# The norms of a hybrid decoder trunk: mean squares spread by one matrix product with a tile of 1/1024

## The reference, cut to what matters

```python
def rmsnorm(x, g):
    xf = x.astype(jnp.float32)
    y = xf * lax.rsqrt(jnp.mean(xf * xf, axis=-1, keepdims=True) + EPS)   # EPS = 1e-6
    return (y * g.astype(jnp.float32)).astype(x.dtype)

for l in range(DEPTH):                                                    # DEPTH = 2
    h = h + 0.5 * swiglu(rmsnorm(h, ffn1_norm[l]), ffn1_w_in[l], ffn1_w_out[l])
    u = rmsnorm(h, mix_norm[l])
    q_a, c_kv, iq, ik, iw, z_pool, q_c, gate_pre = jnp.split(u @ w_in[l], split_pts, axis=-1)
    c_kv = rmsnorm(c_kv, kv_norm[l])                                      # 128 wide
    y_a = dsa_attention(...)      # an indexer scores the keys, top 128 are attended to
    y_b = pool_mixer(...)
    y_c = mem_attention(q_c, rmsnorm(mem, mem_norm[l]), w_mem_kv[l])      # 256 memory tokens
    h = h + (gated sum of the three branches) @ w_out[l]
    h = h + 0.5 * swiglu(rmsnorm(h, ffn2_norm[l]), ffn2_w_in[l], ffn2_w_out[l])
return rmsnorm(h, final_norm)
```

## Time and profile before

| | |
|---|---|
| median of three runs | 2257.93 us (2256.59 to 2258.37) |
| the profiled execution, its own time | 2256.72 us |
| its span in the trace | 2254.9 us |
| PE, matmul busy | 2209.5 us, 98% of the span, 10328 instructions |
| DVE busy | 963.2 us, 43% |
| ACT busy | 548.4 us, 24% |
| POOL busy | 1320.7 us, 59% |
| granted TensorE clock, mean | 0.996 |

### The profile page before, as it was taken

How to read it: one execution, slowest core, us unless ns; L and a number is a source line. 1 busy time by engine, 2 the same in 40 slices (tenths; PEclk the granted TensorE clock), 3 DMA queues, 4 the chain that set the end, 5 groups by cost and what they waited for, 6 DMA issues and landing times.

```text
span 2254.9 us, 31688 instructions
## 1 busy us (share of the span) xinstructions
PE 2209.5 (98%) x10328; PEld 1813.3 (80%) x10328; DVE 963.2 (43%) x1803; ACT 548.4 (24%) x1030; POOL 1320.7 (59%) x868
## 2 busy tenths in 40 slices
PE   7999999999999999999999999999999999999996
PEld 5888888778788888888788888888778888888885
DVE  4331345478754532023433222536877454321334
ACT  3110112443553211001121101215445432100111
POOL 5666667544436666666756666675444366666663
PEclk9999999999999999999999999999999999999998
DMA  6243323221213222322323332232121132323322
GB/s 173 101 131 105 100 77 120 89 71 62 67 56 99 94 93 88 101 100 85 108 98 120 105 110 94 78 121 82 61 71 64 50 112 94 99 83 107 101 78 72
DMA packets 67524, 209.81 MB, mean 93 GB/s; under 512 B 7368, under 2 KB 10600, under 8 KB 67176
## 3 DMA queue, kind: packets, MB, share of 16 engines
q1 hardware_dynamic: 63600, 202.84, 27.4%
q10 hardware_dynamic: 3832, 5.77, 1.1%
HBM read 204.91 MB, written 3.67 MB: 93 GB/s over the span
## 4 chain that ended last, share of the span: by engine, by line
PE 93%; DVE 4%; issue 1%; ACT 1%; DMA 0%; POOL 0%; DVEq 0%; ACTq 0%; POOLq 0%
PE bank L550 29%; PE bank L552 28%; PE bank L551 28%; PE obank L790 1%; PE sbank L735 1%; PE tbank L757 1%; DVE picks L1289 1%; DVE top L1287 1%; PE obank L568 0%; PE obank L562 0%; PE sbank L727 0%; PE sbank L710 0%; PE obank L774 0%; PE sbank L688 0%; PE sbank L741 0%
## 5 line engine op out<-in xcount | busy, mean ns | idle before, releaser
L504 POOL TENSOR_TENSOR wL<-raw,wH 128x1024 fp32r<-128x1024 f32 (+3 forms) x432 | 913.9, 2116 | 36.1
L501 POOL TENSOR_SCALAR wH<-raw 128x1024 fp32r<-128x1024 f32 (+3 forms) x432 | 406.9, 942 | 872.3 <-PE bank L552 858.5
L550 PE MATMUL bank<-u0H,wH 128*128 128x512 f32 x1408 | 551.4, 392 | 6.3 <-POOL wL L504 4.1
L552 PE MATMUL bank<-u0L,wH 128*128 128x512 f32 x1408 | 548.8, 390 | 0.0
L551 PE MATMUL bank<-u0H,wL 128*128 128x512 f32 x1408 | 548.8, 390 | 0.0
L550 PEld LDWEIGHTS bank<-u0H,wH 128*128 128x128 f32 x1408 | 265.0, 188 | 64.8 <-issue 8.7
L551 PEld LDWEIGHTS bank<-u0H,wL 128*128 128x128 f32 x1408 | 264.9, 188 | 55.5 <-issue 1.0
L552 PEld LDWEIGHTS bank<-u0L,wH 128*128 128x128 f32 x1408 | 264.9, 188 | 55.2
L550 PE MATMUL bank<-u1H,wH 128*128 128x512 f32 x704 | 293.3, 417 | 4.7 <-DVE u1L L1488 2.7
L552 PE MATMUL bank<-u1L,wH 128*128 128x512 f32 x704 | 275.2, 391 | 0.0
L551 PE MATMUL bank<-u1H,wL 128*128 128x512 f32 x704 | 274.9, 390 | 0.0
(11 more groups left out here) (174 smaller groups left out, 2140.1 us busy)
## 6 DMA issues: line engine op xcount, KB each, us to landing
raw<-in_wA SPq DMA_DIRECT2D x176, 512.0 KB, 3.2
raw<-in_wM SPq DMA_DIRECT2D x96, 512.0 KB, 3.3
raw<-in_wB SPq DMA_DIRECT2D x64, 384.0 KB, 3.0
raw<-in_wB SPq DMA_DIRECT2D x64, 320.0 KB, 2.9
raw<-in_wR SPq DMA_DIRECT2D x32, 256.0 KB, 2.6
h<-in_xT ACTq DMA_DIRECT2D x4, 512.0 KB, 7.3
mem<-in_memT SPq DMA_DIRECT2D x2, 1024.0 KB, 6.9
near_bias<-bias_rows ACTq DMA_DIRECT2D x2, 1024.0 KB, 7.0
```

The lines of the kernel that those rows point to most:

```text
L501: pool.tensor_scalar(wH[:, w, 0:cols], raw[:, slot, 0:cols], 1.0, 0.0, ALU.mult, ALU.add).then_inc(rounded, 1)
L504: pool.tensor_tensor(wL[:, w, 0:cols], raw[:, slot, 0:cols], wH[:, w, 0:cols].bitcast(F32), ALU.subtract).then_inc(split_done, 1)
L550: pe.matmul(dst, a, hi[:, k, :], start=first and i == 0, stop=False)
L552: mm = pe.matmul(dst, a, lo[:, k, :], start=False, stop=last and i == len(tiles) - 1)
```

## The change

One product takes the place of the two. A tile filled with 1/1024 (over_d; 1/128 for the latents, over_r) is the weights, and ssq itself, 128 x 512, the moving operand, so that obank holds the mean squares of all tokens on every partition. ACT takes the root of the whole 128 x 512 with EPS as a bias, straight into the destination; DVE takes the reciprocal in place and makes the correction with three scalar_tensor_tensor over 128 x 512. Row sums, diagonals and the copy go. Three memsets on DVE at the start fill the constant tiles, and PE and ACT wait for them, ACT before its first DMA of h. In norm 3 the product stands behind unit 1, no longer behind unit 0; in norm 4 it stays behind ("in", 2), but all of DVE's part moves to ("in", 3); in norm 2 all of DVE's part comes before the second half. The diff, cut to its core:

```diff
-            def sum_rows(src, n, cols=T):
+            def mean_square(weights, src, n, cols=T):
                 pe.wait_ge(norm_taken, n)
-                for b in range(cols // P):
-                    mm = pe.matmul(obank[:, b:b + 1], src[:, b * P:(b + 1) * P], ones[:, 0:1], start=True, stop=True)
-                mm.then_inc(norm_sum, 1)
-            def spread(diag, n, cols=T):
-                pe.wait_ge(norm_diag, n)
-                pe.matmul(obank[:, 0:cols], ones, diag[:, 0:cols], start=True, stop=True).then_inc(norm_spread, 1)
+                pe.matmul(obank[:, 0:cols], weights, src[:, 0:cols], start=True, stop=True).then_inc(norm_mean, 1)
...
-                    if i == 0:
+                    if i == 1:
                         pe.wait_ge(ssq_added, l * 24 + 16)
-                        sum_rows(ssq[:, :], l * 5 + 3)
-                    if i == 1:
-                        spread(tb, l * 5 + 3)
+                        mean_square(over_d[:, :], ssq, l * 5 + 3)
...
-                act.activation(norm[:, 1, 0:blocks], norm[:, 0, 0:blocks], ACT.Sqrt).then_inc(norm_root, 1)
+                act.activation(dst, obank[:, 0:cols], ACT.Sqrt, bias=eps[:, 0:1]).then_inc(norm_root, 1)
+            act.wait_ge(weights_set, 3)
...
-            def inverse_rms(n, diag, count, blocks=QB):
-                v, s, r = (norm[:, i, 0:blocks] for i in range(3))
-                dve.wait_ge(norm_sum, n)
-                dve.tensor_scalar(v, obank[:, 0:blocks], 1.0 / count, EPS, ALU.mult, ALU.add).then_inc(norm_var, 1)
+            def inverse_rms(n, dst, cols=T):
+                mean = obank[:, 0:cols]
                 dve.wait_ge(norm_root, n)
-                own.done(dve.reciprocal(r, s))
+                own.done(dve.reciprocal(dst, dst))
                 own.wait()
-                for b in range(blocks):
-                    own.done(dve.tensor_scalar(s[:, b:b + 1], r[:, b:b + 1], r[:, b:b + 1], v[:, b:b + 1], ALU.mult, ALU.mult))
+                own.done(dve.scalar_tensor_tensor(mean, mean, EPS, dst, ALU.add, ALU.mult))
                 own.wait()
-                own.done(dve.tensor_scalar(s, s, -0.5, 1.5, ALU.mult, ALU.add))
+                own.done(dve.scalar_tensor_tensor(mean, mean, -0.5, dst, ALU.mult, ALU.mult))
                 own.wait()
-                for b in range(blocks):
-                    if b == blocks - 1:
-                        own.wait()
-                    ins = dve.tensor_scalar(diag[:, b * P:(b + 1) * P], ident, r[:, b:b + 1], s[:, b:b + 1], ALU.mult, ALU.mult)
...
-            def take_rms(n, dst, cols=T):
-                dve.wait_ge(norm_spread, n)
-                own.done(dve.tensor_copy(dst, obank[:, 0:cols]))
+                own.done(dve.scalar_tensor_tensor(dst, mean, 1.5, dst, ALU.add, ALU.mult))
+                own.wait()
+                dve.sem_inc(norm_taken, 1)
+            dve.memset(over_d[:, :], 1.0 / D).then_inc(weights_set, 1)
+            dve.memset(over_r[:, :], 1.0 / R).then_inc(weights_set, 1)
+            dve.memset(eps[:, :], EPS).then_inc(weights_set, 1)
...
                 mem_kv(0)
-                inverse_rms(l * 5 + 3, tb, D)
                 mem_kv(1)
-                take_rms(l * 5 + 3, rms[:, :])
+                inverse_rms(l * 5 + 3, rms[:, :])
...
                     if at == ("in", 3):
-                        take_rms(l * 5 + 4, ckv_rms)
+                        inverse_rms(l * 5 + 4, ckv_rms)
```

More of the change, by code:

```diff
@@ L248, in trunk @@
         ta = sb("ta", [P, T])
-        tb = sb("tb", [P, T])
+        over_d = sb("over_d", [P, P])
+        over_r = sb("over_r", [P, P])
+        eps = sb("eps", [P, 1])
         sg = sb("sg", [P, 2, T])
         iw = sb("iw", [P, QB, IH])
-        norm = sb("norm", [P, 3, QB])
         top8 = sb("top8", [P, 8])
@@ L587, in ready @@
                                     pe.wait_ge(u_ready, l * 24 + (u_from + k + 1))
-                            within = {3: lambda: spread(tb, l * 5 + norm_n)} if first and i == 2 else None
                             exact(bank[i][:, :], i % 2, [(k, k) for k in range(KD)], u0H, u0L,
-                                  before=ready, within=within).then_inc(unit_used, 1)
+                                  before=ready).then_inc(unit_used, 1)
                             if first and i == 0:
                                 pe.wait_ge(ssq_added, l * 24 + ssq_count)
-                                sum_rows(ssq[:, :], l * 5 + norm_n)
+                                mean_square(over_d[:, :], ssq, l * 5 + norm_n)
                     def outs(u, c, n_hid, hid_chunk):
@@ L618, in ffn @@
                         pe.wait_ge(mem_ssq, l * KD + KD)
-                        sum_rows(ssq[:, 0:M], l * 5 + 2, M)
+                        mean_square(over_d[:, :], ssq, l * 5 + 2, M)
                     with pe.Fori(0, HALF[1] // 2) as j:
                         hidden(j, unit + 40, chunk + 32, False)
-                    if unit == 0:
-                        spread(ssq, l * 5 + 2, M)
                     outs(unit + 60, chunk + 52, HALF[1], chunk + 32)
@@ L839, in _ @@
                         pe.wait_ge(ckv_squared, l + 1)
-                        sum_rows(ckv_sq, l * 5 + 4)
-                    if at == ("in", 3):
-                        spread(tb, l * 5 + 4)
+                        mean_square(over_r[:, :], ckv_sq, l * 5 + 4)
                     if at == ("in", 6):
@@ L874, in _ @@
             pe.wait_ge(ssq_added, L * 24 + 8)
-            sum_rows(ssq[:, :], L * 5 + 1)
-            spread(tb, L * 5 + 1)
+            mean_square(over_d[:, :], ssq, L * 5 + 1)
         @block.scalar
@@ L920, in hidden @@
                                            bank[2 * i + 1][:, :], ACT.Copy).then_inc(hidden_high, 1)
-                    root(l * 5 + root_n)
+                    root(l * 5 + root_n, rms[:, :])
                     with act.Fori(0, HALF[0] // 2) as j:
@@ L957, in _ @@
                 last_half(0, 8, G_MIX, u1H)
-                root(l * 5 + 3)
+                root(l * 5 + 3, rms[:, :])
                 def exps(i):
@@ L1076, in _ @@
                     if at == ("in", 2):
-                        root(l * 5 + 4)
+                        root(l * 5 + 4, ckv_rms)
                         act.preload_act_table_set("natural_log_exp_and_others")
@@ L1115, in _ @@
                 own.restart()
-            root(L * 5 + 1)
+            root(L * 5 + 1, rms[:, :])
         @block.vector
@@ L1192, in hidden @@
                         own.restart()
-                    inverse_rms(l * 5 + norm_n, tb, D)
-                    take_rms(l * 5 + norm_n, rms[:, :])
+                    inverse_rms(l * 5 + norm_n, rms[:, :])
                     own.restart()
@@ L1215, in ffn @@
                     if unit == 0:
-                        inverse_rms(l * 5 + 2, ssq, D, M // P)
+                        inverse_rms(l * 5 + 2, mem_rms[:, :], M)
                         own.restart()
@@ L1511, in _ @@
                 last_half(U_FFN2, 24, G_NEXT, u0H, u0L)
-            inverse_rms(L * 5 + 1, tb, D)
-            take_rms(L * 5 + 1, rms[:, :])
+            inverse_rms(L * 5 + 1, rms[:, :])
             for k in range(KD):
```

24 lines of the change are left out of this document (6 added, 18 removed).

## The result

The changed kernel takes 2299.34 us (median of five runs, 2297.70 to 2301.14), the kernel before 2257.95 beside it (2256.59 to 2259.09). The ratio is 1.0185, 95% interval [1.0174, 1.0196]: 41 us slower, where 3.8 us faster was forecast. The profiled execution is the one of 2301.14 us; its span is 2299.3 us, with a mean granted clock of 0.994 (0.996 before).

What follows compares the result with a forecast made beforehand. PE was taken to bound the kernel (93% of the chain of waits). The terms 0.3 - 3.6 - 0.9 - 4.2 + 3.8 + 0.8 gave -3.8 us, so 2254.1 us on the median, range 2249.0 to 2261.5.

Steps and rivals of the forecast that it cites:

- What a product costs PE: PE's price per norm: steady products 0.23 us apart, new product 0.87 us, removed work 0.89 us per 512-token norm.
- Norm 4: Latents' norm, two in all: DVE's longer chain makes PE wait 2.8 us for the third score; +3.8 us.
- R: Time of DVE's new reciprocal over 128x512, extrapolated from 2 to 4 columns: 3.48 us, three times on the path.
- The estimate of 4.3 us: Alternative reciprocal time from the skill page's repeat count, 8.3 ns a column; would make the sum 2.4 us worse.
- start: Kernel start: three constant-tile memsets on DVE delay ACT's first load of h; +0.3 us, bounds -0.5 to +1.05.
- norm 1: Norms 1 and 5, four in all: only PE's time counts, 0.89 us saved each; -3.6 us.
- norm 2: Two in all, half the columns and records: PE loses 0.45 us of work each; -0.9 us.
- norm 3: Two in all: product behind unit 1 saves the sums and waits, 2.1 us each; -4.2 us.
- last norm: End of the kernel, everything on the path: longer reciprocal and corrections outweigh the removed steps; +0.8 us.
- a cheap reciprocal: Rival: DVE's reciprocal costs 0.70 us like a plain operation; sum -12.2, 2245.7 us; chance 0.18.
- a slow one behind POOL: Rival: reciprocal above 4.2 us puts L1478 behind POOL's subtraction in norm 4; +2.8, 2260.7 us; chance 0.2.
- norm 3 gives only the sums' time: Rival: POOL or DVE is slower there, so 1.2 us of waits stay; sum -1.4, 2256.5 us; chance 0.12.

Runs made afterwards that it cites:

- e1: The changed kernel with an unused tile of 32 bytes a partition in front of u0H; 2256.01 us, ratio 0.9993.
- e2: The kernel before the change with an unused tile of 32 bytes a partition in front of u0H; 2301.74 us, ratio 1.0196.
- e11: The kernel before the change with 32 bytes in front of h, so every tile moves and all distances stay; 2256.85 us, ratio 0.9999.
- e9: e1 without the three corrections in norm 4, which leaves out part of the computation; 2247.24 us, ratio 0.9954.
- e8: e1 with norm 3's product back behind unit 0; 2258.82 us, ratio 1.0006.
- e18: e1 with norm 4's reciprocal before the first low parts, its corrections and ckv scaling behind the fourth score's picks; 2246.15 us, ratio 0.9949.
- e10: e1 with norm 4's reciprocal before the first low parts, its corrections and ckv scaling before the second low parts; 2251.57 us, ratio 0.9975.
- e6: e1 with norm 4's whole DVE chain one unit earlier, in front of the first low parts; 2255.57 us, ratio 0.9994.

## Why the prediction was wrong, point by point

**The step that failed** is the silent one under "What a product costs PE": "In the steady stream the three products of a tile start 0.23 us apart." That number was carried over to the changed kernel for the 6720 products that it doesn't touch. 0.2267 us became 0.2333, because tiles that come and go in SBUF move the others (e1, e2, e11). The allocations stand in the whole kernel, and the diff's core leaves them out; I counted them at nothing and named nothing that would make it so. No rival had it either. The Trainium skill, SBUF — State Buffer (SBUF: two separate sides), names only two places where accesses contend, the port that DVE and GpSimd share and the DMA side; here the place of PE's own two operands cost 43 us. Whether that is accesses contending no run shows; the section gives no reason to expect such a cost, and the measurement decides. The same page of the Trainium skill (Operand start alignment) treats an address as a question of what is allowed, and says that its runs timed nothing.

**Norm 4: +3.8 forecast, +7.4 measured** (3.6 and 3.8 in e1). The wait was right: 2.8 us forecast, 2.92 measured, with the named releaser. Missing was the clock behind it, 1.7 us a layer (e9). The forecast gave a wait on PE its own length only. This alone would have made the forecast too good by 3.6 us and left it inside its range.

**R: 3.48 forecast, 3.353 measured.** The slope over 2 to 4 columns held: (3353 - 1753) / 256 = 6.25 ns a column. The estimate of 4.3 us from the repeat count of 8 in the Trainium skill, VectorE: DVE Perf Modes (First, the fixed hardware budget), is a microsecond too long, and the measurement decides. The reciprocal does take several times as long as a plain operation (3353 ns against 698).

**The rest of the sum held**, read in e1 from PE's landmarks against before:

```
term                    forecast   measured in e1
start                   +0.3       +0.1   (norm 1's product 23.00 for 22.87)
norm 1                  -0.9       -0.95  (norm 5 of layer 0, norms 1 and 5 of layer 1: -0.9 each)
norm 2                  -0.45      -0.47
norm 3                  -2.1       -2.1   (396.28 -> 392.91, of which -1.3 came before it)
last norm               +0.8       +0.7
```

With 7.4 for norm 4 these make some -0.6 us, which is how far e1's profiled execution (2256.08) lies under the one before (2256.72).

Behind unit 1 the product had no wait (e8 put it back and lost 2.8 us, for 2 x 1.2 of waits forecast). Of the rivals, a cheap reciprocal (3.35 us), a slow one behind POOL and "norm 3 gives only the sums' time" were all ruled out by the same rows. With the place restored the kernel takes 2256.0, inside the range; the clock's 3.4 is more than the 1.9 that it lies above 2254.1.

## What to carry to other kernels

When a diff adds or removes an SBUF tile, write down the addresses of the weights' and the moving tiles on both sides: a difference that is no longer a multiple of 256 bytes cost up to 3% of each product of 512 columns here, and an unused tile of 32 bytes gave it back. If a group of instructions that the change doesn't touch has a new mean duration, look there before you look at the schedule. And price a wait of PE of 2 to 3 us at its length and, as a second case, 1.7 us more, since the clock fell behind some such waits here and not behind others; moving DVE's work to where DVE is idle, and behind everything that PE will ask for next, was worth more here (9.9 us from e1 to e18) than the change itself.

## What the runs showed of the hardware that I had not expected

- The pace of 512-column products depends on how the weights' tile and the moving tile lie to one another: 0.2267 us at a distance of a multiple of 256 bytes per partition, 0.2333 at 224, and over the whole kernel +44 us at 32, +19 at 64, +39 at 128, +43 at 192. Moving everything together by 32 bytes costs nothing (e11). The products of 256 columns, with y beside wH and wL, kept their 0.12 us in the changed kernel.
- One of two weight tiles off (wL) costs as much as both (50 and 52 us), and the product that pays most is the one beside which that tile is loaded (402 ns for 392).
- After PE had stood idle for 2.92 us in a full stream the granted clock was 0.50 for some 6 us in layer 0 of the changed kernel, and for some 3.4 in its layer 1 and in both layers of e1. After 1.9 us (e10) it was 0.74 and 0.92 over two stretches of 5 us in layer 0, and 1.00 in layer 1; after 3.3 us in e6 it was 1.00 in layer 0 and 0.66 in layer 1. So the length of the wait alone doesn't tell, and the same wait in the same kernel comes with a fall or without; what decides was not tried.
- The clock also falls in places that the change doesn't touch. In e2, which only moves tiles, the clock was 0.50 from 396 to 398 us, among norm 3's units, where PE had waited 1.4 us for ssq; the kernel before has that wait too (1.25 us), and its profiled execution kept 1.00. Its executions lie between 2255.3 and 2259.5 us, the faster ones with the higher mean clock (0.996 against 0.995 and 0.994), so a difference of a microsecond or two between kernels is read from medians of many executions, or from the rows.
- A reciprocal of 128x512 takes 3353 ns, one of 128x256 1753 ns.
